# A fused state-space, gating and convolution block in f32: readout interleaved with the last gate unit, chunk inputs with the first, the skip term moved into the Toeplitz kernel, its matrix loaded by three queues

## What is computed

```python
y = u * d_skip                                   # skip term, one factor per feature
for direction in range(2):
    h = scan(orient(u), ab, bb, s0=last state of the context)
    y = y + orient(readout(h, c[direction]))
y_a = gelu(y) * sigmoid(gelu(y) @ w_glu + b_glu)
g_a, g_b = split(sigmoid(gate_logits + b_gate))
x = x + ga1 * ((g_a * (y_a @ w_proj_a) + g_b * (y_b @ w_proj_b)) @ w_out)
```

## Time and profile before

| | |
|---|---|
| median of 3 runs | 465.14 us (464.94 to 468.69) |
| the profiled execution | 470.01 us |
| its span from first to last instruction | 468.1 us |
| PE busy in it | 454.2 us (97%) |
| DVE busy in it | 401.3 us (86%) |
| ACT, POOL busy in it | 117.1 us (25%), 45.3 us (10%) |
| mean granted TensorE clock | 0.981 of full speed |

### The profile page before, as it was taken

One profiled execution on the slowest core, in us unless ns is written; L12 is line 12 of the kernel. 1 busy time (PEld: TensorE's weight loads), 2 busy tenths in 40 slices (PEclk: granted clock), 3 DMA queues, 4 the chain that ended last, 5 costly groups with the idle time before them and its releaser, 6 DMA issues.

```text
span 468.1 us, 7678 instructions
## 1 busy us (share of the span) xinstructions
PE 454.2 (97%) x2637; PEld 350.4 (75%) x2637; DVE 401.3 (86%) x818; ACT 117.1 (25%) x216; POOL 45.3 (10%) x73
## 2 busy tenths in 40 slices
PE   8799999998999989999999999999999999999994
PEld 5477856887888878886468888888888887444453
DVE  4669899999999959778855999999999999899744
ACT  5422254235012204300161421222122122200002
POOL 2000020000404123000000110110110111000000
PEclk9889999999999979999999999999999999999998
DMA  8991489941899999999149644654544454400002
GB/s 298 420 417 65 178 277 169 292 160 69 100 157 389 418 396 400 412 358 407 65 178 405 274 127 189 224 200 163 220 170 153 170 179 45 181 0 0 1 0 90
DMA packets 24604, 98.47 MB, mean 210 GB/s; under 512 B 7608, under 2 KB 9280, under 8 KB 16128
## 3 DMA queue, kind: packets, MB, share of 16 engines
q1 hardware_dynamic: 14592, 72.34, 44.2%
q0 software_dynamic: 5056, 18.61, 12.7%
q10 hardware_dynamic: 4928, 7.14, 4.2%
HBM read 95.49 MB, written 2.60 MB: 210 GB/s over the span
## 4 chain that ended last, share of the span: by engine, by line
PE 77%; DVE 15%; DMA 6%; issue 1%; SPq 1%; ACT 0%; DVEq 0%; ACTq 0%
PE bank L752 33%; PE bank L763 12%; PE bank L569 11%; DVE s_region L1048 8%; PE bank L663 6%; PE bank L707 5%; PE bank L483 4%; DMA s_region<-early_w 4%; DMA s_region<-up_w 2%; PE bank L644 2%; PE bank L684 1%; DVE s_region L1167 1%; PE bank L448 1%; DVE s_region L1305 1%; DVE s_region L1336 1%
## 5 line engine op out<-in xcount | busy, mean ns | idle before, releaser
L752 PE MATMUL bank<-h_all,s_region 128*128 128x256 f32 x704 | 152.3, 380 | 0.2 <-ACT h_all L962 0.2
L752 PEld LDWEIGHTS bank<-h_all,s_region 128*128 128x128 f32 x704 | 133.5, 190 | 18.8 <-ACT h_all L962 0.6
L1567 DVE SCALAR_TENSOR_TENSOR ctx_region<-ctx_region,pk_sb 128x189 f32<-128x189 f32 (+2 forms) x352 | 130.1, 443 | 0.3 <-DVE ctx_region L1567 0.2
L569 PE MATMUL bank<-h_all,ring_region 128*128 128x256 f32 x256 | 58.2, 390 | 0.1
L569 PEld LDWEIGHTS bank<-h_all,ring_region 128*128 128x128 f32 x256 | 49.9, 196 | 7.8 <-issue 0.6
L763 PE MATMUL bank<-s_region,ring_region 128*128 128x512 f32 (+1 forms) x132 | 47.9, 522 | 0.3 <-DMA s_region<-up_w 0.3
L763 PEld LDWEIGHTS bank<-s_region,ring_region 128*128 128x128 f32 x132 | 25.1, 190 | 22.8 <-issue 20.5
L980 ACT ACTIVATE ctx_region<-bank 128x512 f32<-128x512 f32 x22 | 13.1, 597 | 113.3 <-PE bank L752 60.1
L1048 DVE TENSOR_TENSOR s_region<-s_region,power 128x2048 f32<-128x2048 f32 (+1 forms) x16 | 38.1, 2420 | 0.2
L396 POOL TENSOR_TENSOR ring_region<-gates,ctx_region 128x256 f32 x22 | 17.3, 786 | 178.1 <-ACT gates L988 178.1
L483 PE MATMUL bank<-h_all,ring_region 128*128 128x256 f32 x128 | 33.1, 407 | 0.0
(11 more groups left out here) (242 smaller groups left out, 529.3 us busy)
## 6 DMA issues: line engine op xcount, KB each, us to landing
s_region<-up_w SPq DMA_DIRECT2D x33, 1024.0 KB, 4.9
ring_region<-ring_w SPq DMA_DIRECT2D x20, 1024.0 KB, 9.8
s_region<-mod_w POOLq DMA_DIRECT2D x20, 512.0 KB, 14.7
s_region<-early_w SPq DMA_DIRECT2D x4, 1024.0 KB, 21.7
s_region<-out_w SPq DMA_DIRECT2D x4, 1024.0 KB, 13.2
gates<-mod_w ACTq DMA_DIRECT2D x8, 512.0 KB, 5.4
gates<-early_w SPq DMA_DIRECT2D x2, 1024.0 KB, 10.7
s_region<-k_scratch POOLq DMA_DIRECT2D x8, 256.0 KB, 11.9
```

Of the source, the lines that this page charges most:

```text
L569: mx = pe.matmul(bank[5 - j % 2][:, mm * TOK:(mm + 1) * TOK], ring[:, u % RING, (mm * KD + k) * P:(mm * KD + k + 1) * P], h_x[:, k, :], st ...
L752: mx = pe.matmul(bank[s % 3][:, half * TOK:(half + 1) * TOK], up_ring[:, s, (half * KD + k) * P:(half * KD + k + 1) * P], h2[:, k, :], sta ...
L1567: dve.scalar_tensor_tensor(out=o, in0=a, scalar=cw[:, tile[half], (dy + 1) * 3 + dx + 1], in1=o, op0=ALU.mult, op1=ALU.add).then_inc(s_con ...
```

## The change

- **Readout and last gate unit.** The readout is cut into four parts of 32 matmuls (`carried`, by `g2` and direction), gate unit 7 into four quarters of 4 (`last_gate_part`), and they alternate. ACT copies each of the two banks when it is complete.
- **Chunk inputs and first gate unit.** Gate unit 0 is cut into two halves; the second stands between jobs 1 and 2 of the chunk inputs.
- **Skip term.** `skip_eye` (the factor on a 16x16 identity, made by DVE in place of the copy `u_x`) is added by DVE to lag 0 of `k_sb`, before the evacuation of job 7. The store of `k_sb` waits for it. DVE's eight operations after the transposes go, and ACT's gelu reads PSUM in two halves.
- **Toeplitz loads.** POOL loads `tau` 0, 2, 4, ACT 1, 3, 5, SP 7, 6. ACT waits for the store and issues before its sigmoids of gate unit 1; SP before it loads the weights of gate unit 5, and its loop over ring loads is written out. POOL waits for all eight, as before.
- **Smaller ones.** The transposition of ga1 on PE moves behind the GLU and projection 3; the sums of tiles 16 to 19 move behind y_a; the two multiplications of a merge become one over 512 elements.

```diff
+        def load_toeplitz(q, tau, count):
+            q.dma_start(m_toep[tau * H:(tau + 1) * H, :, :],
+                        k_dram[:, :, (T - 1 - tau) * H:(2 * T - 1 - tau) * H].rearrange("m (g h) n -> h (m g) n", h=H)).then_inc(count, 16)
...
-            full = U_GLU // RING
-            with sp.Fori(2, full) as i:
...
+            for u in range(2 * RING, UNITS):
+                if u == U_GATE + 5:
+                    sp.wait_ge(s_k_out, 16)
+                    for tau in (7, 6):
+                        load_toeplitz(sp, tau, s_m_hw)
                 sp.wait_ge(s_unit, u - RING + 1)
...
-            for tau in range(T):
-                pool.dma_start(m_toep[tau * H:(tau + 1) * H, :, :],
...
+            for tau in (0, 2, 4):
+                load_toeplitz(pool, tau, s_m)
...
-            gate_unit(0)
+            gate_unit(0, (0,))
...
             for job in range(E_BANKS):
+                if job == 2:
+                    gate_unit(0, (1,))
...
-            pe.wait_ge(s_scan, 1)
-            for g2 in range(2):
...
-            gate_unit(7)
+            pe.wait_ge(s_scan, 1)
+            carried(0, 0)
+            ring_ready(pe, U_GATE + GATES - 1)
+            pe.wait_ge(s_gate, 2 * (GATES - 2))
+            last_gate_part(0, 0)
+            carried(0, 1)
+            last_gate_part(0, KD // 2)
+            carried(1, 0)
+            last_gate_part(1, 0)
+            carried(1, 1)
+            last_gate_part(1, KD // 2)
...
-            act.wait_ge(s_k, 2)
+            chunk_inputs_copied(6)
+            act.wait_ge(s_k_skip, 1)
             act.dma_start(k_dram[:].rearrange("m p n -> p m n"), k_sb[:, :].rearrange("p (m n) -> p m n", m=KS)).then_inc(s_k_out, 16)
-            chunk_inputs_copied(6)
+            act.wait_ge(s_k_out, 16)
+            for tau in (1, 3, 5):
+                load_toeplitz(act, tau, s_m_hw)
...
-            act.wait_ge(s_y, 2 * KS)
-            act.activation(y_gelu.rearrange("p m (c t) -> p m t c", t=T), y_feat, ACT.Gelu_apprx_tanh).then_inc(s_ygelu, 1)
+            for b in range(2):
+                act.wait_ge(s_y_tr, b + 1)
+                act.activation(y_gelu.rearrange("p m (c t) -> p t m c", t=T)[:, 4 * b:4 * b + 4],
+                               bank[b][:, :].rearrange("p (t m c) -> p t m c", t=4, m=KS), ACT.Gelu_apprx_tanh).then_inc(s_ygelu, 1)
...
-            dve.wait_ge(s_uf, KS)
-            dve.tensor_copy(u_x[:, :].rearrange("p (m c) -> p m c", c=CH), u_feat.rearrange("p m t c -> p (m t) c")[:, :, CH:2 * CH]).then_inc(s_ux, 1)
+            dve.wait_ge(s_pk2, 16)
+            tt(skip_eye, par("eye_h").unsqueeze(1).broadcast_to([P, KS, H]), par("s5_d").unsqueeze(2).broadcast_to([P, KS, H]), ALU.mult)
...
             for job in (3, 4, 5, 7):
+                if job == 7:
+                    dve.wait_ge(s_k, 2)
+                    dve.tensor_tensor(k_lag0, k_lag0, skip_eye, ALU.add).then_inc(s_k_skip, 1)
...
-            for b in range(2):
-                dve.wait_ge(s_y_tr, b + 1)
-                y_ps = bank[b][:, :].rearrange("p (t m c) -> p m t c", t=4, m=KS)
-                for m in range(KS):
-                    dve.scalar_tensor_tensor(out=y_feat[:, m, 4 * b:4 * b + 4], in0=u_x[:, m * TOK:(m + 1) * TOK].rearrange("p (t c) -> p t c", t=T)[:, 4 * b:4 * b + 4],
...
-            modulation_sums(12, 18)
+            modulation_sums(12, 16)
...
-            modulation_sums(18, 20)
+            modulation_sums(16, 18)
```

More of the change, by code:

```diff
@@ L191, in build @@
         a_raw = sb("a_raw", 3 * DP)
+        skip_eye = a_raw[:, 0:KS * H].rearrange("p (m h) -> p m h", m=KS)
         small = sb("small", 16 * DP)
@@ L199, in build @@
         k_sb = m_region[:, 0:KS * LAGS * H]
+        k_lag0 = k_sb.rearrange("p (m j h) -> p m j h", m=KS, j=LAGS)[:, :, T - 1, :]
         def par(name):
@@ L318, in _ @@
                              u_dram[:, :, tau, :].rearrange("m (g h) c -> h (m g) c", h=H)).then_inc(s_uchunk, 16)
-            full = U_GLU // RING
-            with sp.Fori(2, full) as i:
-                for s in range(RING):
-                    sp.wait_ge(s_unit, i * RING + (s - RING + 1))
-                    sp.dma_start(ring[:, s, :], ring_w[bass.ds(i * RING + s, 1)].rearrange("a p n -> p (a n)")).then_inc(s_ring[s], 16)
-            for u in range(full * RING, UNITS):
+            for u in range(2 * RING, UNITS):
[3 more added lines that the diff above has]
+                        load_toeplitz(sp, tau, s_m_hw)
                 sp.wait_ge(s_unit, u - RING + 1)
@@ L560, in chunk_inputs, with gate_unit @@
                 mx.then_inc(s_e_ps, 1)
-            def gate_unit(j):
+            def gate_unit(j, halves=(0, 1)):
                 u = U_GATE + j
@@ L566, in gate_unit @@
                     pe.wait_ge(s_gate, 2 * (j - 1))
-                for mm in range(2):
+                for mm in halves:
                     for k in range(KD):
@@ L570, in gate_unit @@
                                        h_x[:, k, :], start=(k == 0), stop=(k == KD - 1))
-                mx.then_inc(s_unit, 1)
+                if halves[-1] == 1:
+                    mx.then_inc(s_unit, 1)
             pe.wait_ge(s_win, 16)
-            gate_unit(0)
+            gate_unit(0, (0,))
             pe.wait_ge(s_uchunk, 16 * T)
@@ L635, in _, with carried @@
             gate_unit(6)
-            pe.wait_ge(s_scan, 1)
-            for g2 in range(2):
+            def carried(g2, d):
                 half = slice(g2 * N, (g2 + 1) * N)
-                for d, r, e0 in ((0, 0, 1), (0, 1, 1), (1, 0, 0), (1, 1, 0)):
+                for r in range(2):
                     for j in range(P // H // 2):
@@ L644, in _, with last_gate_part @@
                             mx = pe.matmul(bank[g2][m * CH:(m + 1) * CH, j * P:(j + 1) * P], carry[half, (r * 2 + d) * PAIRS + q, :],
-                                           ca[half, d, r, q, e0:e0 + T, :].rearrange("p e h -> p (e h)"),
+                                           ca[half, d, r, q, 1 - d:1 - d + T, :].rearrange("p e h -> p (e h)"),
                                            start=False, stop=(d == 1 and r == 1), skip_group_check=True)
-                mx.then_inc(s_y8_ps, 1)
-            gate_unit(7)
+                if d == 1:
+                    mx.then_inc(s_y8_ps, 1)
+            def last_gate_part(mm, k0):
+                u = U_GATE + GATES - 1
+                for k in range(k0, k0 + KD // 2):
+                    mx = pe.matmul(bank[4][:, mm * TOK:(mm + 1) * TOK], ring[:, u % RING, (mm * KD + k) * P:(mm * KD + k + 1) * P],
+                                   h_x[:, k, :], start=(k == 0), stop=(k == KD - 1))
+                if mm == 1 and k0 > 0:
+                    mx.then_inc(s_unit, 1)
+            pe.wait_ge(s_scan, 1)
[9 more added lines that the diff above has]
+            last_gate_part(1, KD // 2)
             pe.wait_ge(s_y8, 2)
@@ L1742 @@
     pk = np.concatenate(_features(a["c"][0], a["c_ctx"], a["b_ada"][0], a["g_mix"][0]) + [pick]
[L1743 removed]
+                        + _features(a["g_ffn"][0], a["b_gate"][0], a["s5_b_glu"][0], a["s5_d"][0], a["conv_b"][0]) + [conv_w, np.tile(np.eye(H, dtype=np.float32), (P // H, 1))], axis=1)
     def per_state(v):
```

47 lines of the change are left out of this document (20 added, 27 removed).

## The result

The changed kernel takes 471.64 us in the median of five runs (467.49 to 472.18), the one before 465.14 beside it (464.69 to 468.69). The ratio is 1.0092, 95% interval 1.0054 to 1.013. The medians of the first series are 6.5 us apart, more than the ratio says, because the five runs of the changed kernel lie in two groups (467.5 to 468.3 and 471.6 to 472.2). I had forecast 461.1 us with a range of 459.2 to 464.6: by the ratios the change makes the kernel some 3 to 4 us slower where I had it 4 us faster.

What follows compares the result with a forecast made beforehand. PE was taken to bound the kernel from 117 us on; 470.01 - 3.2 - 0.45 - 0.3 = 466.0 us profiled, and the same 4.0 off the median 465.14 gave 461.1 us, range 459.2 to 464.6.

Steps and rivals of the forecast that it cites:

- What bounds the kernel: From 117 us on, shortening PE's stream moves the end by as much, unless another engine or load comes up behind.
- Term 1: Readout interleaved with gate quarters: pause and slow clock go, the stretch falls from 18.42 to 15.2 us; -3.2 us.
- Term 2: DVE ahead of gate unit 1: skip_eye replaces the copy u_x, and the chunk-input pause goes; -0.45 us.
- Term 3: Wait for y_a: two modulation tiles fewer stand before it on DVE; -0.3 us, bounds 0 and -0.3.
- edit (b): DVE's eight operations after the transposes (2.2 us) were hidden before the GLU, so removing them was costed at nothing.
- the Toeplitz loads: Three queues run side by side at 110 GB/s each, all landed near 130 us; no term, only room.
- edit (d): ACT waits for the store of k_sb, which lands 2.8 us later because of the add; costed at nothing.
- The rival that ended slower: Queues share 110 GB/s, gate unit 5's ring load comes late, PE idles 6.0 us: 467.1 us; chance 0.06.
- a clock fall behind an idle stretch: If PE idles for gate unit 5's late ring load and the clock falls there: about 470 us instead of 467.1.

Runs made afterwards that it cites:

- e5: The kernel before, unchanged, traced a second time: span 466.9 us.
- e3: Changed kernel with the readout and gate unit 7 each in one piece: 470.27 us, 1.008 of the kernel before.
- e10: Changed kernel with the skip add before chunk job 3, nothing interleaved and all Toeplitz loads on POOL: 464.67 us, 0.9947 of the kernel before.
- e6: Kernel before with only the readout's parts interleaved with the quarters of gate unit 7: 466.08 us, 0.9987 of the kernel before.
- e7: Changed kernel with the skip add before chunk job 3, readout and gate unit 7 each in one piece: 461.82 us, 0.9884 of the kernel before.
- e4: Changed kernel with the skip add before the evacuation of chunk job 3 instead of job 7: 462.41 us, 0.9917 of the kernel before.
- e12: Kernel before with four of DVE's modulation sums ahead of y_a in place of six: 465.62 us, 0.9991 of the kernel before.
- e9: Changed kernel with the skip add before chunk job 3 and gate unit 0 whole ahead of the chunk inputs: 461.89 us, 0.9907 of the kernel before.
- e13: Changed kernel with ring loads from gate unit 5 on held until the Toeplitz matrix is in, three queues: 470.52 us, 1.0036 of the kernel before.
- e11: Changed kernel, unchanged, timed and traced again: 468.78 us, 1.0063 of the kernel before.
- e8: Changed kernel with the skip add before chunk job 3 and all Toeplitz loads on POOL: 464.05 us, 0.9914 of the kernel before.
- e14: Changed kernel with ring loads held until the Toeplitz matrix is in, all Toeplitz loads on POOL: 472.81 us, 1.0082 of the kernel before.
- e1: Changed kernel with DVE's sums of modulation tiles 12 to 15 moved behind y_a: 465.97 us, 0.9992 of the kernel before.
- e2: Changed kernel with all eight Toeplitz loads on POOL's queue: 469.56 us, 1.008 of the kernel before.

## Why the prediction was wrong

**What bounds the kernel: wrong, and at the root.** I read "PE without a break from 117 us on" off the chain of one execution. In it the readout ran at the low clock for some microseconds, just long enough to hide that the gelu and y_a waited for DVE's sums and these for loads. Its only trace was 0.32 us of idle time before y_a and gelu's end 1.05 us ahead of the GLU. e5 has waits of 3.5 and 1.5 us there. What I took as "any microsecond saved on PE is saved in the end" held only up to those places.

**Term 1, readout, -3.2.** The changed stretch came out as worked out: 14.9 us (forecast 15.2), clock 1.00, no pause, so that the time between two fetches, read from two places, was good enough; that the pauses are fetches stays my reading. What was wrong is the 18.42 that it was set against: e3, e5 and e10 have 14.5 to 14.6 in the old order. Removing the pause of 0.8 to 0.95 and adding three pairs of changes comes to 0.3 to 0.4 us more, not less. What is left is cover against a clock fall that came in three of six traces and costs some 3.6 us, and in the kernel before that fall was hidden by the loads. e6 and e7 against e4 measure nothing.

**Term 2, -0.45: right.** Gate unit 1 starts at 111.7 to 111.9 us in the changed kernel where no early fall precedes it, at 112.25 in e6 and 112.5 in e12, with DVE deciding. The pause in the chunk inputs went as forecast, but had no part in it: with the pause back, e9 starts at 112.0.

**Term 3, -0.3, and edit (b).** Right cause, wrong size. The wait of 0.32 before y_a and the cover over the eight operations were both residues of the slow readout. By e5 and e6 the new path of the gelu takes out 3.1 to 3.5 us ahead of the GLU, and two sums fewer take 1 MB, about 3.3 us, out of the run of loads. In e4 y_a starts 73.7 us behind gate unit 1 where it was 77.2 to 77.9 before, and this is where its -3.9 us come from. What each of the two is worth alone, no run shows. That my forecast of -4.0 equals e4's is chance: its terms are not these.

**The step that failed: the Toeplitz loads.** The prediction had "three loads into different partitions at once may run side by side", all landed near 130 and `c_row` near 131, so the store's delay in edit (d), which I had seen and put at 2.8 us, could be costed at nothing. Measured, the first Toeplitz load, which goes out when the store has landed, went from 0.8 to 5.2 us behind gate unit 1; then the three queues moved 212 GB/s in the first window (118 to 120 us) and 101 to 146 in the next three. They took 26.25 us (before 25.9), and e13 gives 123 GB/s for the three even with nothing beside them. The 110 GB/s a queue that I had assumed was there for the first 2 us only. The earlier trace rows has two kinds of load with one rate, and I gave it to the 16 partitions; but both rows also have the DMA share at 1.04 or more, which should have made me doubt that there was room for more. The share alone does not settle it: in the first window it is 1.07 at 212 GB/s. The Trainium skill ("Trainium Kernel Development and Optimization", Key Constraints) says that issuing from several engines "only saves the sequencer's issue time"; by these runs it is nearer than my reading: 95 against 123 GB/s over the whole of the loads, not three times.

**The rival that ended slower** had the right premise, queues that share about one rate, and the wrong victim. The ring load of gate unit 5 was not late; the loads of `mod_w` behind were, and with them y_a. I had written of them only that they would start sooner. The added wait's queue I followed on ACT and SP; what stood behind the loads on POOL and DVE I did not.

**The rest of the loss.** PE's pause of 4.2 us before y_a is followed by a clock fall that costs 1.7 us of the +2.6 here and 3.0 of the +2.9 in e11; the segments around it differ by under 0.6 us each. I had priced a clock fall behind an idle stretch at 3 us, but for the ring load alone.

## What to carry to other kernels

Before a chain of waits is trusted to say that an engine bounds a stretch, look for small idle times released by something else (here 0.3 us before y_a): with a slow clock in the same trace, the other bound may stand right behind it, and a second trace costs little. Where the DMA engines show a share of 1.0 over a long stretch, count the bytes from its start to what is waited for at its end. Here 22.3 to 23.5 MB went at 311 to 322 GB/s. A store that goes out later moves all behind it, fewer bytes ahead of what is waited for shorten it, and more queues gave 0.2 us with the early store and 2.3 with the late one. An operation put between a copy and its store belongs as early in its engine's program as its operands allow: one line placed three evacuations too late turned a gain of 4 us into a loss of 3.

Of the versions run, e4, e7, e8, e9 and e10 beat both kernels. e4, e7 and e9 have the lowest medians (461.8 to 462.4 us, 0.988 to 0.992 of before), but the intervals of the five overlap. I would keep e4 or e9, where the quarters of gate unit 7 keep the clock up in the readout.

## What the runs showed of the hardware that I had not expected

- Loads of 256 KB into 16 partitions moved 95 GB/s from one queue (e14) and 123 from three (e13), at a busy share of the DMA engines of 1.03 and 1.16, while the loads of `mod_w` and the ring move about 400 at the same share. In their first 2 us ACT's and SP's loads moved 212 GB/s at 1.07. So a busy share of 1 does not say how much is moved. Why the rate falls after 2 us, no run shows.
- The store of 480 KB took 2.9 to 3.1 us where the add came early (e4, e7 to e10), 3.4 to 3.8 in the kernel before, and 4.5 to 5.1 where the add came late (after, e1 to e3, e11, e13, e14). In the changed kernel it moves 360 GB/s from 113 to 114 us and 31 and 22 in the two windows behind, with a busy share of 0.13 and 0.07; what it waits for there, no run shows.
- The granted clock falls at one place in some executions of a kernel and not in others: half of the six traces with the readout in one piece, none of ten with large matmuls between. Behind PE pauses it fell in after, e11, e2, e3 and e14 (4.2 to 7.8 us) and did not in e5, e6 and e13 (1.4 to 3.5 us). What decides, these runs do not settle.
